# Respacing modulation pairs, reordering an opening and taking norm roots through TensorE in a two-layer decoder kernel

## The reference

```python
mod = silu(c) @ ada_w + ada_b            # 1024 x 6144 per layer: shift, scale, gate, twice
h = rmsnorm(x, norm_g[0]) * (1 + scale1) + shift1
z = h @ w_in                             # chunk MLP, short conv, 31-tap conv, 3 x 1024 gates
merged = sum over 3 branches of gate * (y @ w_branch)
x = x + gate1 * (merged @ w_out)
h2 = rmsnorm(x, norm_g[1]) * (1 + scale2) + shift2
x = x + gate2 * peer(h2)                 # product keys, 16384 experts swept densely for most tokens
y = rmsnorm(x, final_g)                  # at the end
```

## Time and profile before

| what | us |
|---|---|
| median of three runs | 3975.6 |
| the profiled execution | 3977.77 |
| its span, first to last instruction | 3976.1 |
| TensorE busy (98% of the span) | 3878.4 |
| VectorE busy (69%) | 2743.4 |
| ScalarE busy (40%) | 1582.8 |
| mean granted TensorE clock | 0.991 |

### The profile page before, as it was taken

How to read it: one execution, slowest core, us unless ns; L and a number is a source line. 1 busy time by engine, 2 the same in 40 slices (tenths; PEclk the granted TensorE clock), 3 DMA queues, 4 the chain that set the end, 5 groups by cost and what they waited for, 6 DMA issues and landing times.

```text
span 3976.1 us, 76076 instructions
## 1 busy us (share of the span) xinstructions
PE 3878.4 (98%) x29028; PEld 3802.3 (96%) x29028; DVE 2743.4 (69%) x4476; ACT 1582.8 (40%) x2673; POOL 817.9 (21%) x689
## 2 busy tenths in 40 slices
PE   7999999999999999999999999899999999999998
PEld 5989989999999999999989899899999999999998
DVE  4478479877666537777755774897766664587776
ACT  3222433333677633333332233333347775333332
POOL 1000000000222225555210000000002221455551
PEclk8999999999999999999999999999999999999999
DMA  6453322544566679999834522235446667799995
GB/s 230 124 147 121 136 95 87 179 137 137 157 194 194 187 239 345 346 349 352 305 117 107 165 86 91 75 115 167 138 133 176 194 194 213 251 351 346 349 348 189
DMA packets 418219, 781.86 MB, mean 197 GB/s; under 512 B 151184, under 2 KB 274448, under 8 KB 417344
## 3 DMA queue, kind: packets, MB, share of 16 engines
q1 hardware_dynamic: 176640, 441.70, 34.6%
q10 hardware_dynamic: 194240, 196.10, 15.5%
q0 software_dynamic: 47104, 141.00, 10.0%
HBM read 655.79 MB, written 122.88 MB: 196 GB/s over the span
## 4 chain that ended last, share of the span: by engine, by line
PE 83%; DVE 7%; ACT 6%; issue 1%; DMA 1%; SPq 0%; ACTq 0%; DVEq 0%; POOLq 0%
PE pg L1611 17%; PE pg L1614 16%; PE pg L1612 16%; PE pm L1933 5%; PE pg L1934 5%; PE pm L1934 5%; PE pm L1935 5%; PE pg L1933 5%; PE pg L1935 5%; ACT one_j L959 3%; DVE w_lo L1041 2%; DVE ys L1252 2%; ACT w_hi L934 1%; DVE one_j L1502 1%; PE pm L1886 1%
## 5 line engine op out<-in xcount | busy, mean ns | idle before, releaser
L1611 PE MATMUL pg<-a_hi,w_hi 128*128 128x260 f32 x6400 | 1682.0, 284 | 21.7 <-DVE a_lo L1072 16.2
L1612 PE MATMUL pg<-a_lo,w_hi 128*128 128x260 f32 x6400 | 1669.2, 283 | 0.0
L1041 DVE TENSOR_TENSOR w_lo<-raw,w_hi 128x1024 fp32r<-128x1024 f32 x688 | 841.0, 1224 | 940.4 <-ACT w_hi L934 701.9
L1614 PE MATMUL pg<-a_hi,w_lo 128*128 128x260 f32 x6400 | 1289.8, 283 | 0.0
L1611 PEld LDWEIGHTS pg<-a_hi,w_hi 128*128 128x128 f32 x6400 | 1209.7, 189 | 37.4 <-issue 31.1
L1612 PEld LDWEIGHTS pg<-a_lo,w_hi 128*128 128x128 f32 x6400 | 1206.6, 189 | 0.1
L1614 PEld LDWEIGHTS pg<-a_hi,w_lo 128*128 128x128 f32 x6400 | 988.0, 189 | 0.0
L934 ACT CAST w_hi<-raw 128x1024 fp32r<-128x1024 f32 x499 | 524.7, 1051 | 780.7 <-PE pg L1935 734.4
L606 POOL DMA_INDIRECT rows<-stream,at_v x256 | 283.2, 1106 | 765.8 <-DVE acc_tok L1536 316.4
L616 POOL TENSOR_TENSOR one_j<-one_j,g_lo 128x896 fp32r<-128x896 f32 x112 | 189.8, 1695 | 1043.2 <-ACTq L962 1043.2
L654 ACT ACTIVATE hid<-pg 128x260 f32<-128x260 f32 x512 | 170.7, 385 | 509.9 <-PE pg L1614 488.0
(11 more groups left out here) (247 smaller groups left out, 5397.0 us busy)
## 6 DMA issues: line engine op xcount, KB each, us to landing
raw<-stream SPq DMA_DIRECT2D x688, 512.0 KB, 3.9
hidden_dram<-hid SPq DMA_DIRECT2D x256, 196.0 KB, 3.5
gate_dram<-gate_buf ACTq DMA_DIRECT2D x28, 1792.0 KB, 10.7
hid_in<-hidden_dram ACTq DMA_DIRECT2D x64, 784.0 KB, 6.0
gate_in<-gate_dram ACTq DMA_DIRECT2D x64, 784.0 KB, 11.0
ada_raw<-stream ACTq DMA_DIRECT2D x76, 512.0 KB, 4.2
hid_tok<-hid SPq DMA_DIRECT2D x256, 64.0 KB, 3.5
rows<-stream,at_v POOLq DMA_INDIRECT x256, 7.4
```

The lines of the kernel that those rows point to most:

```text
L1041: tt(ring(False, s), raw[:, s], ring(True, s).bitcast(F32), ALU.subtract).then_inc(lo_ready, 1)
L1611: pe.matmul(outs[h], w[0], a[h][0], start=first, stop=False)
L1612: pe.matmul(outs[h], w[0], a[h][1], start=False, stop=False)
L1614: mm = pe.matmul(outs[h], w[1], a[h][0], start=False, stop=last)
```

## The change

1. **Places of the pairs.** In layer 0 OWN_PAIRS has T_BB + 1 and then T_BR + 0, 2, 5, 7, 10, 12, 15, 17, 20; NEXT_PAIRS has T_BR + 25, 28, 31, 34. In layer 1 the pairs sit at 3, 9, 11, 13, T_BB + 1, T_BR + 0, 3, 6, 9, 12. The last four pairs of each layer's list are run in the gap of the second norm (GAP_2), two between the two square sums and two after them. The first of the four uses `ada_raw`, the other three six tiles held in `ys`, which ScalarE loads during steps T_O to T_O + 2. Pairs that follow a step's product go from 37 to 30; those in a second norm's gap from 1 to 8. `ada_turn` of the first of the two batches there runs in the gap, of the second behind the first queries' products. The load of `keys` also waits for the last of these pairs.
2. **Norm sums.** `square_sum` is four matmuls into four strips of 32 partitions, each for a quarter of the tokens (130). One root and one reciprocal of 128 x 130 follow. `spread_roots` brings them back to all partitions: four matmuls whose stationary operand is one column of `ident`, broadcast, so that PSUM columns 200 to 459 of two banks hold the 520 roots. `scaled`, the samples' products and the final scaling read them there, `scaled` over 520 tokens instead of 512; the samples have a tile of their own.
3. **The opening.** The root's table is loaded early; the order of sums, turns and `ada_rows` on TensorE and ScalarE is changed; the first pair's load comes ahead of the casts; `prompt(0)` comes between the second and third cast.

```diff
-OWN_PAIRS = (3, 5, 7, 9, 11, 13, T_BB + 1, T_BB + 3, *range(T_BR, T_BR + 16, 2))
 GAP_1, GAP_2 = T_V + 1, T_O + KC
-NEXT_PAIRS = (*range(T_BR + 25, T_O, 2), T_O, GAP_2)
-TILE_STEP = {4 * FIRST_BATCHES + n: (0, w) for n, w in enumerate(w for w in OWN_PAIRS for _ in range(2))}
-for _l in range(1, DEPTH):
-    TILE_STEP |= {4 * BATCHES * _l + n: (_l - 1, w) for n, w in enumerate(w for w in NEXT_PAIRS for _ in range(2))}
-    TILE_STEP |= {4 * BATCHES * _l + 2 * len(NEXT_PAIRS) + n: (_l, w) for n, w in enumerate(
-        (GAP_1,) * 4 + tuple(w for w in OWN_PAIRS[0:1] + OWN_PAIRS[3:] for _ in range(2)))}
-assert 2 * (len(OWN_PAIRS) + len(NEXT_PAIRS)) == NMOD and sorted(TILE_STEP) == list(range(4 * FIRST_BATCHES, NMOD * DEPTH))
-RAW_TILES = [g for g in sorted(TILE_STEP) if TILE_STEP[g][1] != GAP_1]
+OWN_PAIRS = (3, 5, 7, 9, 11, 13, T_BB + 1, *(T_BR + n for n in (0, 2, 5, 7, 10, 12, 15, 17, 20)))
+NEXT_PAIRS = tuple(T_BR + n for n in (25, 28, 31, 34))
+LAST_PAIRS = (3, 9, 11, 13, T_BB + 1, *(T_BR + n for n in (0, 3, 6, 9, 12)))
+
+
+def steps_of(pairs):
+
+    return [w for w in pairs for _ in range(2)]
+
+
+assert DEPTH == 2
+TILE_STEP = {4 * FIRST_BATCHES + n: at for n, at in enumerate(
+    [(0, w) for w in steps_of(OWN_PAIRS + NEXT_PAIRS) + [GAP_2] * KC] + [(1, w) for w in [GAP_1] * 4 + steps_of(LAST_PAIRS) + [GAP_2] * KC])}
+assert sorted(TILE_STEP) == list(range(4 * FIRST_BATCHES, NMOD * DEPTH))
+AT_GAP_2 = [[g for g in sorted(TILE_STEP) if TILE_STEP[g] == (l, GAP_2)] for l in range(DEPTH)]
+assert all(a[0] % 4 == 0 for a in AT_GAP_2)
+HELD = KC - 2
+RAW_TILES = [g for g in sorted(TILE_STEP) if TILE_STEP[g][1] != GAP_1 and not any(g in a[2:] for a in AT_GAP_2)]
 GROUPS = 4
 CW = P // GROUPS
+QT, SPREAD = T // GROUPS, 200
...
+        def spread_to(nth):
+            return (pm[:, 0:2] if nth % 2 or nth == 2 * DEPTH else pg[:, 0])[:, :, SPREAD:SPREAD + HT]
+
+        def halves(t):
+            return t.rearrange("p (h t) -> p h t", h=2)
...
+        held_tiles = ys[:, :, :, :].rearrange("p a b t -> p (a b t)")[:, 0:HELD * KC * P].rearrange("p (n k m) -> p n k m", n=HELD, k=KC)
...
+                pool.wait_ge(ada_used, AT_GAP_2[l][-1] + 1)
...
-                for h in range(2):
-                    act.activation(rstd[:, h * HT:(h + 1) * HT], pm[:, h, 0:HT], ACT.Sqrt, bias=eps_t[:, 0:1], scale=scale).then_inc(std_ready, 1)
+                act.activation(rstd[:, 0:QT], pm[:, 0, 0:QT], ACT.Sqrt, bias=eps_t[:, 0:1], scale=scale).then_inc(std_ready, 1)
...
-                if 0 < b < FIRST_BATCHES:
+                if b:
...
+            def load_held(l, n):
+
+                act.wait_ge(y_ready, (l + 1) * 3)
+                act.sem_inc(passed, 1)
+                layer, at = divmod(AT_GAP_2[l][2 + n], NMOD)
+                act.dma_start(held_tiles[:, n], stream[layer * (NMOD + NT) + at]).then_inc(held_in, 16)
...
+                    prompt(0, 1)
+                    split(l, 0, 2)
+                    split(l, 0, 3)
+                    for k in range(1, 4):
...
+                    prepare_roots()
                     ada_rows(0)
+                    std(l, 0, 1.0 / D)
                     ada_rows(1)
-                    std(l, 0, 1.0 / D)
-                    for k in range(4):
-                        split(l, 0, k)
+                    ada_rows(2)
                     for g in loads_first(0):
                         load_ada(g)
-                    ada_rows(2)
+                    split(l, 0, 0)
+                    split(l, 0, 1)
...
+                    if k < HELD // 2:
+                        load_held(l, 2 * k)
+                        load_held(l, 2 * k + 1)
...
+                ada_rows(AT_GAP_2[l][0] // 4)
                 modulate(l, 1)
-                ada_after(l, GAP_2)
+                ada_rows(AT_GAP_2[l][4] // 4)
...
-                for h in range(2):
-                    dve.wait_ge(std_ready, nth * 2 + h + 1)
-                    own.do(dve.reciprocal(rstd[:, h * HT:(h + 1) * HT], rstd[:, h * HT:(h + 1) * HT]))
-                own.settle()
+                dve.wait_ge(std_ready, nth + 1)
+                own.link(dve.reciprocal(rstd[:, 0:QT], rstd[:, 0:QT]))
+                dve.sem_inc(root_made, 1)
...
                 def scaled(k):
-                    dve.scalar_tensor_tensor(out=merged[:, k, 0:SEQ], in0=x[:, k, 0:SEQ], scalar=mod_scale[:, w, k, 0:1],
-                                             in1=rstd[:, 0:SEQ], op0=ALU.mult, op1=ALU.mult).then_inc(nb_ready, 1)
+                    dve.scalar_tensor_tensor(out=halves(merged[:, k, :]), in0=halves(x[:, k, :]), scalar=mod_scale[:, w, k, 0:1],
+                                             in1=roots, op0=ALU.mult, op1=ALU.mult).then_inc(nb_ready, 1)
...
+                dve.wait_ge(root_spread, l * 2 + w + 1)
                 if l == 0 and w == 0:
-                    for k in range(4):
+                    scaled(0)
+                    take_ada(2)
+                    for k in range(1, 4):
                         scaled(k)
-                        if k:
-                            split(l, k - 1, k - 1)
-                    take_ada(2)
-                    scaled(4)
+                    split(l, 0, 0)
+                    split(l, 1, 1)
                     low(0, 1)
+                    split(l, 2, 2)
                     split(l, 3, 3)
                     for k in range(1, 4):
                         low(k, k + 1)
-                        scaled(k + 4)
+                        scaled(k + 3)
+                    scaled(7)
...
-                for h in range(2):
-                    mm = pe.matmul(pm[:, h, 0:HT], ones[:, :], square[:, h * HT:(h + 1) * HT], start=g == 0, stop=g == len(groups) - 1)
+                for n in range(GROUPS):
+                    mm = pe.matmul(pm[n * CW:(n + 1) * CW, 0, 0:QT], ones[:, 0:CW], square[:, n * QT:(n + 1) * QT],
+                                   start=g == 0, stop=g == len(groups) - 1)
                 mm.then_inc(sq_used, 1)
+
+            def spread_roots(nth):
+
+                pe.wait_ge(root_made, nth + 1)
+                if nth == 0:
+                    pe.wait_ge(mod_taken, 3)
+                for n in range(GROUPS):
+                    mm = pe.matmul(spread_to(nth)[:, n // 2, n % 2 * QT:(n % 2 + 1) * QT], ident[:, n * CW:n * CW + 1].to_broadcast([P, P]), rstd[:, 0:QT],
+                                   start=True, stop=True)
+                mm.then_inc(root_spread, 1)
...
+                if g in RAW_TILES:
+                    for z in range(2):
+                        pe.wait_ge(ada_in[z], (RAW_TILES.index(g + z) // 2 + 1) * 16)
+                    in_groups(out, lambda k: ada_raw[:, :, k, :]).then_inc(ada_used, 2)
+                else:
+                    l = TILE_STEP[g][0]
+                    n = AT_GAP_2[l].index(g) - 2
+                    pe.wait_ge(held_in, (l + 1) * HELD * 16)
...
                     first_ada(0)
                     first_ada(1)
                     square_sum(l, 0, 0)
+                    ada_turn(0)
                     first_ada(2)
+                    ada_turn(1)
+                    spread_roots(0)
+                    ada_turn(2)
                     first_ada(3)
...
                     ada_step(l, GAP_1)
+                    spread_roots(l * 2)
...
-                pe.wait_ge(std_ready, l * 4 + 2)
...
                 square_sum(l, 1, 0)
-                ada_step(l, GAP_2)
+                for g in AT_GAP_2[l][0:4:2]:
+                    ada_pair(g)
                 square_sum(l, 1, 1)
+                for g in AT_GAP_2[l][4:8:2]:
+                    ada_pair(g)
+                spread_roots(l * 2 + 1)
+                ada_turn(AT_GAP_2[l][0] // 4)
...
-                ada_step(l, GAP_2 + 1)
+                ada_turn(AT_GAP_2[l][4] // 4)
                 scores(l, 0, 0)
-                if l + 1 < DEPTH:
-                    pe.wait_ge(mod_taken, (l + 1) * BATCHES + FIRST_BATCHES + 1)
+                pe.wait_ge(mod_taken, batches_by(l, T_EU) + 1)
...
+            spread_roots(2 * DEPTH)
```

38 lines of the change are left out of this document (19 added, 19 removed).

## The result

| | before | changed |
|---|---|---|
| median, us | 3977.73 (4 runs) | 3950.22 (4 runs) |
| lowest to highest | 3975.41 to 3980.54 | 3947.36 to 3953.65 |
| the profiled execution | 3977.77 | 3947.52 |
| TensorE busy | 3878.4 | 3867.8 |

Ratio **0.9929**, 95% interval 0.9916 to 0.9943: faster by 0.7%, beyond the 0.2% that by the prediction's own figure a measurement tells from nothing. The forecast said 3945.5 for the median, in a range of 3936 to 3958, and 3947.7 for the profiled execution. The median is 4.7 above the forecast; the profiled execution took 3947.5. The sum fits that execution better than its terms do, as the rest shows. Two executions further down took far longer at a lower granted clock, one of a_late (7084 us at 0.831) and one of the kernel before beside best (4429 us at 0.802), and the medians given leave them out.

A forecast was written before the change was run, and what follows sets the result against it. TensorE, busy 3878.4 of 3976.1 us, was taken as the bound. Terms 10.4 - 2.6 + 0.5 + 12.5 + 3.0 + 2.0 + 2.8 + 1.5 gave 30.1 us off, a median from 3975.6 to 3945.5, range 3936 to 3958.

The forecast's parts named there:

- Pairs and turns: Seven pairs moved into the second norms' gaps and three turns fewer in TensorE's stream: gain 10.4 us.
- the late tiles: Two TensorE waits for modulation tiles (`ada_raw`), one a layer, go as the pair comes a step later: gain 12.5 us.
- what is given back: Without the pair at T_BR + 27, the wait for the third branch's y grows to 2.3 us: loss 2.6.
- up to 3.5 of idle time is filled (I take 2): Second branch, layer 0: two more pairs there fill TensorE's waits for VectorE's taps; 2 us taken.
- up to 1.5: Possible extra loss if the longer wait for the third branch's y halves TensorE's clock for a while.
- The convolution becomes the bound: Rival, chance 0.10: savings before the second branch's end return as waits for VectorE; gain 11, 3964.5 us.
- a band of -3 to +3.5: Bounds on idle time filled or returned by VectorE's taps in the second branch, both layers; net +0.5 us taken.
- The second norms: Roots to first scaling shrinks from 4.04 to 3.1 us, second sum ends 0.6 sooner: 1.5 each, 3.0 together.
- Reading PSUM: Scalings read the roots from PSUM without surcharge; the skill's figure would mean 1.6 us less gain.
- First norm of layer 1: First scaling 1.2 us sooner, plus 0.8 for a shorter slow-clock stretch: gain 2.0.
- The final norm: Strip sums end with VectorE's adds, 1.5 us; roots to scaling falls from 4.04 to 2.7, 1.3: gain 2.8.
- The opening: Modulations ready some 7 us sooner, limited by weight tiles and the earlier `ada_raw` load: gain 1.5, bounds 0 and 3.

The follow-up runs named there:

- a_late: Changed kernel with its pair at T_BR + 0 put back to T_BB + 3 in both layers; 3966 us, ratio 0.9969.
- best: Changed kernel with a_warm (which includes a_keys), a_load, taps moved, and fillers ahead of the first v products, U and third y's products; 3930.19 us, ratio 0.9879.
- after_again: The changed kernel itself, run and profiled once more; 3951.06 us, ratio 0.9933.
- b_space: Kernel before with only the pair at T_BB + 3 moved to T_BR + 16; 3965.45 us, ratio 0.9967.
- b_nostore: Kernel before without the four stores per layer of the samples' convolution state (`hc_s`); 3978.33 us, one execution alone.
- a_keys: Changed kernel with the load of `keys` no longer waiting for the last `a_lo`; 3948.75 us, ratio 0.9925.
- a_taps: Changed kernel with 29 of the long convolution's 31 taps in each channel block; 3952.17 us, ratio 0.9937.
- a_warm: a_keys plus unread filler matmuls of ones ahead of the queries, in layer 1's first norm and in the final norm; 3946.95 us, ratio 0.9921.
- a_order: Changed kernel with seven taps of the long convolution moved to other steps of VectorE's list, none left out; 3945.19 us, ratio 0.992.
- a_load: Changed kernel with layer 0's first two modulation loads issued behind the rounding of the fourth v tile; 3949.33 us, ratio 0.9932.
- a_root: Changed kernel with the norms' sums, roots and reciprocals as two halves, as before, without the roots' spread; 3961.02 us, ratio 0.9962.

## Why the prediction was right, and where it was not

**Pairs and turns, the late tiles, what is given back.** Forecast 10.4 - 2.6 + 0.5 + 12.5 = 20.8; by the milestones 6.4 + 3.2 + 7.9 + 1.8 = 19.3, of which up to 2.9 is the clock's favour in that one execution (after_again). The tile waits are the best-tested term: b_space measures 12 to 13. The reason given for the lateness was half of it. That "the small stores of the convolution's state push it" names one cause; the second, a load sent late behind ScalarE's wait for `src_ready`, the forecast did not see, and by b_nostore a change that only took the stores away would have gained nothing.

In layer 0 the term "up to 3.5 of idle time is filled (I take 2)" failed: TensorE's waits of over 0.4 us for VectorE up to and at the sums are 4.7 us (2.34, 0.70, 1.08, 0.62) where they were 4.9. Behind the sums 3.2 were gained for 1.6. The wait for the third y is 2.26, as worked out (2.3), but the "up to 1.5" for the clock did not come in this profile; in a_keys, a_taps, a_warm and a_order it did, a slow stretch there in each, so in those executions the full loss of 2.6 is right.

Layer 1 fell short: 7.9 against 11.45. Of that 1.5 were lost ahead of the fourth sources (a slow stretch at 2031.1 behind the wait of 2.2 for `w_lo`, where the kernel before had the same wait and no slow stretch), and 2 in the branches: waits for VectorE there are 5.0 + 1.8 us, where the kernel before had 3.1 + 1.8. The 1.8 gained behind the sums (a slow stretch at 2396.8 gone) was in no term.

**"The convolution becomes the bound"** (rival, 0.10): its gain of 11 is far from the measured 27.5, and a_taps shows that the end of the taps costs TensorE only 0.6 and 1.8 us at the sums. But the waits it argued from are real, and a_order shows that the longest of them come from the order of VectorE's list. The forecast treated them as a band of -3 to +3.5 without asking which instruction stood ahead of the release.

**The second norms.** 1.5 forecast, 2.0 measured, each part near its term: root 0.37 (0.35), reciprocal 0.97 (0.9), spread 1.16 (1.15). The step that failed is "the last two pairs are still on TensorE for 0.4": the spread begins at 523.85, 0.11 behind the reciprocal's end, so they cost nothing. That the clock "is worth nothing here, since `keys` ends last" was right only for 0.5 us: with `keys` early and the clock held (a_warm) the stretch to the scores is 16.3, 2.2 and 2.5 less. By those two runs the clock's part is 1.6 and 2.2.

**Reading PSUM.** No surcharge, as the row had said: 748 and 750 ns with the roots in PSUM, 755 with all in SBUF. The 62 cycles that the Trainium skill's "VectorE: DVE Perf Modes", section on the TRN2 errata, puts between the two sources do not show in this operation.

**First norm of layer 1.** 1.0 by the sums and roots (1.2 forecast), 1.2 by a shorter slow stretch (0.8): 2.2 against 2.0. In after_again that stretch has its old length, and the gain from it is 0.4 instead of 1.2.

**The final norm.** 1.4 against 2.8, the term most wrong. "In strips they end with the adds" failed: the sums end at 3933.82, 1.2 behind the adds. And roots to scaling take 3.7 instead of 2.7, of which the spread, priced at 1.15, takes 2.10. The timeline:

```profile
3931.87 0.43 PE L1686 MATMUL pm<-merged,ones 128*32 128x130 f32 x8 [1.83 <-DVEq L1169]
3932.72 1.10 PE L1686 MATMUL pm<-merged,ones 128*32 128x130 f32 x16 [0.42 <-DVEq L1169]
3934.36 0.97 DVE L1097 RECIPROCAL rstd<-rstd 128x130 f32<-128x130 f32 x1 [1.75 <-ACT rstd L696]
3935.44 2.10 PE L1696 MATMUL pm<-rstd,ident 128*128 128x130 f32 x8 [1.62 <-DVEq L1098]
3937.58 5.42 DVE L1645 SCALAR_TENSOR_TENSOR x<-x,fin_g,pm 128x520 f32<-128x520 f32 x8 [2.25 <-PE pm L1696]
```

Work made shorter leaves TensorE idle between its pieces (1.83, 0.42, 1.62), its clock falls (0.50 from 3932.3 on), and the pieces take nearly double: the last sums 1.10, the spread 2.10. In a_warm, with fillers between them and the clock at 1.00, they take 0.65 and 1.16, and the stretch is 7.04, the 2.8 of the forecast. The forecast took the price of TensorE's new part from a gap in which it stays busy.

**The opening.** 2.2 against 1.5, but 0.7 of it at the first product and 1.5 behind it, where the slow stretch is 6.8 us long instead of 10.2. The casts of the third and fourth tile slid, the fourth by 3.3 us against the earlier trace rows, and a_load gets 2.2 back. With that agrees what the Trainium skill's "DMA: Bandwidth & Descriptors", section on queues and rings, says of engines that take turns between queues.

**The bounds.** "Its own bounds give gains of 20 to 39" is added up wrongly at its lower end: the lower bounds of all terms make 14.8, the upper ones 39.3.

**Left open.** The sweeps over the experts, which nothing in the change touches, are 1.2 and 0.4 us shorter. With the old roots a_root is 0.8 longer than the changed kernel in layer 0; no run looked for the cause.

## What to carry to other kernels

When a wait goes, look at what is queued behind it on *every* engine that issues something for the next step: the stall of this kernel had two causes in series, and removing the first moved the wait to the next pair without changing the time. When an engine waits for another, read which instruction stands ahead of the release before calling the other engine the bound; seven operations moved behind the release gave 5 us, and eight left out where nothing waited for long gave none. And price a short piece of TensorE's work by what TensorE did just before it: between pauses of 0.4 to 1.8 us such pieces took 1.7 and 1.8 times as long here.
